# Hand-written instruction orders changed at six places of a two-block transformer kernel

## The reference

```python
# first block
h = h + 0.5 * swiglu(rmsnorm(h, ffn1_norm), ffn1_w_gate, ffn1_w_up, ffn1_w_down)   # hidden width 2816
u = rmsnorm(h, mix_norm)
(fq, fk, fv, ff, dq, dk, dv, iq, ik, iw, mq, g) = split(u @ w_in)
o_a = fox_attention(norm(fq), norm(fk), fv, log_sigmoid(ff + b_forget))   # 8 heads of 64, forget gates
o_b = dsa_attention(rope(norm(dq)), rope(norm(dk)), dv, rope(iq), rope(ik), iw, k_sel=128)
o_c = memory_attention(norm(mq), km, vm)       # 4 heads of 128; km, vm from 256 memory rows
h = h + sum_n(sigmoid(g_n) * (o_n @ w_branch[n])) @ w_out
h = h + 0.5 * swiglu(rmsnorm(h, ffn2_norm), ffn2_w_gate, ffn2_w_up, ffn2_w_down)
# second block
p = rms_norm(h, norm_mix_pre) @ w_in_2         # qa, ka, va, qb, kb, vb; 8 query heads, 2 key heads each
mixed = concat(group_norm(global_attention(qa, ka, va)), group_norm(window_attention(qb, kb, vb, sink)))
h = h + rms_norm(mixed @ w_out_2, norm_mix_post)
h = h + rms_norm(swiglu(rms_norm(h, norm_ffn_pre), w_gate_2, w_up_2, w_down_2), norm_ffn_post)
```

## Time and profile before

| | us |
|---|---|
| median of 3 runs (lowest, highest) | 2039.42 (2037.93, 2040.73) |
| the profiled execution, its own time | 2040.19 |
| its span in the trace | 2038.4 |
| PE busy, share of the span | 1960.4, 96% |
| POOL busy, share | 1468.2, 72% |
| DVE busy, share | 949.7, 47% |
| ACT busy, share | 516.1, 25% |

### The profile page before, as it was taken

How to read it: one execution, slowest core, us unless ns; L and a number is a source line. 1 busy time by engine, 2 the same in 40 slices (tenths; PEclk the granted TensorE clock), 3 DMA queues, 4 the chain that set the end, 5 groups by cost and what they waited for, 6 DMA issues and landing times.

```text
span 2038.4 us, 25930 instructions
## 1 busy us (share of the span) xinstructions
PE 1960.4 (96%) x8919; PEld 1597.9 (78%) x8919; DVE 949.7 (47%) x1196; ACT 516.1 (25%) x941; POOL 1468.2 (72%) x1676
## 2 busy tenths in 40 slices
PE   7999999999999999999999999999999989999998
PEld 5788888777677887887788888886778768888886
DVE  6532340488666469656432331017775574323101
ACT  3211100244345342333211110012555441111001
POOL 5777777778666667856777777766665768777776
PEclk9999999999999999999999999999999989999999
DMA  5333323232211223212333332324010013333332
GB/s 170 93 93 98 98 93 98 74 87 84 72 43 53 73 63 93 73 32 63 93 93 93 95 100 94 101 83 103 21 29 24 21 52 100 95 95 100 103 102 74
DMA packets 256183, 164.45 MB, mean 81 GB/s; under 512 B 30204, under 2 KB 245310, under 8 KB 255982
## 3 DMA queue, kind: packets, MB, share of 16 engines
q1 hardware_dynamic: 254304, 157.90, 26.6%
q10 hardware_dynamic: 1806, 5.58, 0.8%
HBM read 161.33 MB, written 2.13 MB: 80 GB/s over the span
## 4 chain that ended last, share of the span: by engine, by line
PE 80%; DVE 9%; POOL 4%; issue 3%; ACT 2%; ACTq 1%; DMA 0%; DVEq 0%; POOLq 0%
PE bank L920 12%; PE bank L922 12%; PE bank L921 12%; PE bank L1222 4%; PE bank L1223 4%; PE bank L1224 4%; PE bank L1040 4%; PE bank L1041 4%; PE bank L1042 4%; POOL w_lo L703 2%; PE bank L1118 2%; PE bank L1035 2%; PE bank L1036 2%; PE bank L1037 2%; DVE work L2582 2%
## 5 line engine op out<-in xcount | busy, mean ns | idle before, releaser
L703 POOL TENSOR_TENSOR w_lo<-raw,w_hi 128x256 fp32r<-128x256 f32 x1088 | 866.3, 827 | 22.7
L699 POOL TENSOR_SCALAR w_hi<-raw 128x1024 fp32r<-128x1024 f32 x272 | 294.5, 1083 | 356.0 <-PE bank L922 153.6
L920 PE MATMUL bank<-u_hi,w_hi 128*128 128x512 f32 x1040 | 407.8, 392 | 3.8 <-DVE u_lo L2436 2.9
L921 PE MATMUL bank<-u_lo,w_hi 128*128 128x512 f32 x1040 | 405.7, 390 | 0.0
L922 PE MATMUL bank<-u_hi,w_lo 128*128 128x512 f32 x1040 | 405.7, 390 | 0.0
L920 PEld LDWEIGHTS bank<-u_hi,w_hi 128*128 128x128 f32 x1040 | 195.8, 188 | 47.0 <-issue 4.2
L921 PEld LDWEIGHTS bank<-u_lo,w_hi 128*128 128x128 f32 x1040 | 195.9, 188 | 41.4 <-issue 0.7
L922 PEld LDWEIGHTS bank<-u_hi,w_lo 128*128 128x128 f32 x1040 | 195.8, 188 | 40.6
L1222 PE MATMUL bank<-u_hi,w_hi 128*128 128x512 f32 x464 | 193.9, 418 | 2.7 <-POOL w_lo L703 1.4
L1223 PE MATMUL bank<-u_lo,w_hi 128*128 128x512 f32 x464 | 183.3, 395 | 0.0
L1224 PE MATMUL bank<-u_hi,w_lo 128*128 128x512 f32 x464 | 183.2, 395 | 0.0
(11 more groups left out here) (555 smaller groups left out, 3573.3 us busy)
## 6 DMA issues: line engine op xcount, KB each, us to landing
raw<-in_w_in SPq DMA_DIRECT2D x52, 512.0 KB, 3.7
raw<-in_ffn_w_gate SPq DMA_DIRECT2D x44, 512.0 KB, 3.8
raw<-in_ffn_w_up SPq DMA_DIRECT2D x44, 512.0 KB, 3.8
raw<-in_ffn_w_down SPq DMA_DIRECT2D x44, 512.0 KB, 3.4
raw<-in_w_gate SPq DMA_DIRECT2D x22, 512.0 KB, 3.8
raw<-in_w_up SPq DMA_DIRECT2D x22, 512.0 KB, 3.8
raw<-in_w_down SPq DMA_DIRECT2D x22, 512.0 KB, 3.3
raw<-in_w_branch SPq DMA_DIRECT2D x12, 512.0 KB, 3.5
```

Source lines behind the costliest of these rows:

```text
L699: pool.tensor_scalar(w_hi[:, s, :], raw[:, k, :], 1.0, 1.0, ALU.mult, ALU.mult).then_inc(hi_done, 1)
L703: pool.tensor_tensor(w_lo[:, s, c], raw[:, k, c], w_hi[:, s, c].bitcast(F32), ALU.subtract).then_inc(low_quarter if quarter < 3 else split ...
L920: pe.matmul(outs[:, 0:n], wh, rhs_hi[:, c, :], start=(c == 0), stop=False)
L921: pe.matmul(outs[:, 0:n], wh, rhs_lo[:, c, :], start=False, stop=False)
```

## The change

Six places of the order change; the arithmetic stays, and so do nearly all instructions.

1. **Last pair of the down projection** (first and second feed-forward). The order over (m, k) was (4..7, 0), then (0, 0), (0, 1), (1, 0), (1, 1), (2, 0), (2, 1), (3, 0), (3, 1), then (4..7, 1). Now it is (4, 5, 6, 7, 0, 1; 0), (0, 1), (2, 0), (3, 0), then (1..7; 1). A product with k = 1 waited for its whole weight tile, and now waits for the quarter that it reads. In the first feed-forward the last two `m_lo` wait for one more finished unit.
2. **Memory slots.** In slots 2 and 3 `by_cos` and `both` of the single key move from between the low halves to behind the next slot's maxima and diagonal. Six of the eight cleared half tiles move from slot 2 to the end of slot 0.
3. **Branch and output projection.** `dsa_branch` takes its first sixteen products with two outputs x ahead of the two others. `w_out_a` takes its units one after the other and no longer interleaves the first two. `mix_lo` lies in another place, over `o_lo`, so that it does not lie where `u_lo` of chunks 4 to 7 is written, and those are made as their residuals come. The feed-forward behind it waits for `res` 6 and no longer 8.
4. **Second block's first panels.** Three products of qa0 stand between chunk 5 and chunk 6 of ka. On DVE the reciprocal for a1 stands ahead of `value_low`.
5. **Second block's attention.** `both` of a3 and of a4 stand ahead of the reciprocal of their step; PE's hook 13 is now 12, and 17 is now 18; ACT's and DVE's pieces for a4 move along.
6. **Third feed-forward's start.** The matmuls of chunk 0 that need only u_hi come first, in both panels, and the second panel follows one chunk behind, no longer two. DVE makes `u_lo` of chunk 0 and 1 earlier, between the residual additions.

The rows below are an engine's instructions in program order, with the line, the operation, out<-in and what it waits for.

DVE, memory slot 3, before: `m_kl` and `m_vl` are low halves that PE waits for, `prep_tmp` is by_sin's result, `rowmax` are the maxima.

The diff, cut to its changed lines (left out: the forget sums on ACT wait for 3 cleared groups, and the second place where `mix_lo` is indexed by `MIX_LO`):

```diff
@@ -246,7 +246,8 @@
-        mix_lo = at("mix_lo", [P, KC, S], u_at + 24576, F32R)
+        mix_lo = at("mix_lo", [P, 12, S], o_at, F32R)
+        MIX_LO = 0, 1, 2, 3, 8, 9, 10, 11
@@ -982,14 +983,26 @@
-                for c in range(KC):
+
+                def first_chunk():
+                    pe.wait_ge(n_hi, SPLITS[ni] * KC + 1)
+                    for k in range(2):
+                        weights(u + k, 0)
+                        b, slot = bank[banks[k]], slots[k]
+                        pe.matmul(b[:], w_hi[:, slot, 0:P], u_hi[:, 0, :], start=True, stop=False)
+                        pe.matmul(b[:], w_lo[:, slot, 0:P], u_hi[:, 0, :], start=False, stop=False)
+                    pe.wait_ge(n_lo, SPLITS[ni] * KC + 1)
+                    for k in range(2):
+                        pe.matmul(bank[banks[k]][:], w_hi[:, slots[k], 0:P], u_lo[:, 0, :], start=False, stop=False)
+                first_chunk()
+                residual_turned(0)
+                for c in range(1, KC):
...
-                        chunk(1, c - 2)
+                        chunk(1, c - 1)
                     residual_turned(c)
-                for c in range(KC - 2, KC):
-                    chunk(1, c)
+                chunk(1, KC - 1)
@@ -1064,13 +1077,16 @@
-                    order = [(m, 0) for m in range(4, KC)] + [(m, k) for m in range(4) for k in range(2)]
-                    order += [(m, 1) for m in range(4, KC)]
+                    order = [(m, 0) for m in (4, 5, 6, 7, 0, 1)] + [(0, 1), (2, 0), (3, 0)]
+                    order += [(m, 1) for m in range(1, KC)]
...
-                        pe.wait_ge(split_ready, d0 + FT)
                         pe.wait_ge(f_lo, fi * FT + FT)
+                        if fi == 2:
+                            pe.wait_ge(split_ready, d0 + FT)
+                    if k and fi < 2:
+                        weights(d0 + FT - 1, m)
@@ -1521,10 +1537,11 @@
-                for c in range(4):
+                order = [(x, c) for c in range(3) for x in range(2)] + [(2, 0), (3, 0), (0, 3), (1, 3)]
+                order += [(x, c) for c in range(1, 4) for x in (2, 3)]
+                for x, c in order:
                     pe.wait_ge(o_split, c + 1)
-                    for x in range(4):
-                        branch_mm(16 + x, c, bank[banks[x]][:])
+                    branch_mm(16 + x, c, bank[banks[x]][:])
@@ -1534,35 +1551,29 @@
-                b, slot = bank[m], m % SPL
+                b, slot = bank[m % 4], m % SPL
...
-                pe.matmul(b[:], wh, mix_lo[:, c, :], start=False, stop=False)
+                pe.matmul(b[:], wh, mix_lo[:, MIX_LO[c], :], start=False, stop=False)
...
-                pe.wait_ge(b_add, 16)
-                for c in range(KC - 2):
-                    pe.wait_ge(b_lo, c + 1)
-                    mix_mm(0, c)
-                for c in range(KC - 2):
-                    mix_mm(1, c)
-                for c in range(KC - 2, KC):
-                    pe.wait_ge(b_lo, c + 1)
-                    mix_mm(0, c)
-                for c in range(KC - 2, KC):
-                    mix_mm(1, c)
-                for m in range(2, KC):
-                    if m >= 4:
+                for m in range(KC):
+                    if m < 4:
+                        pe.wait_ge(b_add, 9 + (0, 1, 4, 5)[m])
+                    else:
                         pe.wait_ge(res, m - 3)
-                    panel(U_WO + m, m % SPL, m % 4, (mix_hi, mix_lo))
+                    for c in range(KC):
+                        if m == 0:
+                            pe.wait_ge(b_lo, c + 1)
+                        mix_mm(m, c)
...
-            pe.wait_ge(res, KC)
+            pe.wait_ge(res, KC - 2)
@@ -1624,9 +1635,13 @@
+                query = b2_panel("qa0")
+                next(query)
                 for c in b2_panel("ka"):
+                    if c == KC - 2:
+                        go_on(query, 3)
                     first_key(c)
-                for c in b2_panel("qa0"):
+                for c in query:
@@ -1680,8 +1695,8 @@
-                    13: lambda: aux_free("a3", lambda: sum_a(4, AUX)),
-                    17: lambda: (pe.wait_ge(h_std, H_B2 + 5), turn_a(4)),
+                    12: lambda: aux_free("a3", lambda: sum_a(4, AUX)),
+                    18: lambda: (pe.wait_ge(h_std, H_B2 + 5), turn_a(4)),
...
@@ -2357,9 +2372,8 @@
-                    14: lambda: (std_a(4, AUX), load_exp()),
-                    13: lambda: copy_b(2),
-                    18: lambda: high_a(4),
+                    13: lambda: (copy_b(2), std_a(4, AUX), load_exp()),
+                    19: lambda: high_a(4),
@@ -2700,6 +2714,8 @@
+                    if j == 2:
+                        dve.wait_ge(unit_done, U_GU1 + 3 * FT - 3)
@@ -2773,10 +2789,7 @@
-                by_cos, by_sin, both = rope_parts(R_PREP + j, x, 0, cos1[:], sin1[:], prep_tmp[:], x)
-                by_sin()
-                by_cos()
-                both()
+                return rope_parts(R_PREP + j, x, 0, cos1[:], sin1[:], prep_tmp[:], x)
@@ -2786,7 +2799,8 @@
-                    turn_key(i - 2)
+                    by_cos, by_sin, both = turn_key(i - 2)
+                    by_sin()
@@ -2818,8 +2832,8 @@
-                empty_halves(fst, ("qh", "ql", "kh", "kl")).then_inc(c_one, 1)
-                dve.wait_ge(c_one, 1)
+                empty_halves(fst, ("qh",)).then_inc(c_one, 1)
+                dve.wait_ge(c_one, 2)
@@ -2835,9 +2849,15 @@
+                if i >= 2:
+                    by_cos, by_sin, both = turn_key(i - 2)
+                    by_cos()
+                    both()
...
+                    dve.wait_ge(h_out, H_DK + 1)
+                    empty_halves(fst, ("ql", "kh", "kl")).then_inc(c_one, 1)
...
@@ -3042,10 +3062,9 @@
-                if 1 <= m <= 4:
+                if m:
                     gained_low(N_F2, G_F2, m - 1)
-            for c in range(4, KC):
-                gained_low(N_F2, G_F2, c)
+            gained_low(N_F2, G_F2, KC - 1)
@@ -3118,10 +3137,14 @@
+                dve.wait_ge(h_std, H_B2 + 2)
+                dve.reciprocal(HEAD_SQ[1], HEAD_SQ[1]).then_inc(h_rec, 1)
...
-                norm_a(1)
+                dve.wait_ge(h_rec, H_B2 + 2)
+                dve.scalar_tensor_tensor(out=raw_x[:, X_OF[1], :], in0=raw_x[:, X_OF[1], :], scalar=gain[:, G_QA:G_QA + 1],
+                                         in1=HEAD_SQ[1], op0=ALU.mult, op1=ALU.mult).then_inc(h_out, 1)
@@ -3170,16 +3193,16 @@
-                    (11, "end"): a3[2],
+                    (11, "start"): a3[2],
...
-                    (17, "mid"): a4[0],
-                    (17, "end"): a4[1],
-                    (18, "mid"): a4[2],
-                    (18, "end"): lambda: low_a(4),
+                    (18, "mid"): a4[0],
+                    (18, "end"): a4[1],
+                    (19, "start"): a4[2],
+                    (20, "start"): lambda: low_a(4),
@@ -3266,19 +3289,26 @@
-            for c in range(2):
-                b = bank[7 - 3 * c]
-                gained(c, b[:])
+
+            def added(c):
                 dve.wait_ge(n_t, SCALED[N_POST] * KC + c + 1)
-                dve.tensor_tensor(hT[:, c, :], hT[:, c, :], b[:], ALU.add).then_inc(x_ready, 1)
-            for c in range(2, KC + 3):
+                dve.tensor_tensor(hT[:, c, :], hT[:, c, :], bank[7 - 3 * c][:], ALU.add).then_inc(x_ready, 1)
+            gained(0, bank[7][:])
+            added(0)
+            gained(1, bank[4][:])
+            gained_low(N_FPRE, G_FPRE2, 0)
+            added(1)
+            gained(2, W[4])
+            gained_low(N_FPRE, G_FPRE2, 1)
+            gained(3, W[5])
+            third_square(1)
+            for c in range(4, KC + 3):
                 if c < KC:
-                    if c >= 4:
-                        dve.wait_ge(x_pool, c - 3)
+                    dve.wait_ge(x_pool, c - 3)
...
-                if c - 3 >= 1:
+                if c - 3 >= 2:
```

4 lines of the change are left out of this document (2 added, 2 removed).

## The result

| | before | after |
|---|---|---|
| median of 3 runs, us | 2039.42 (2037.93 to 2040.73) | 2023.24 (2019.71 to 2023.26) |
| the profiled execution | 2040.19 | 2023.26 |
| its span | 2038.4 | 2021.4 |

The account below looks back on a forecast made before the run. PE's matmul list was taken as the bound, with only its idle time and half clock removable. 1.9 + 6.3 + 4.8 + 3.8 + 3.2 + 1.2 = 21.2 gave a forecast of 2018.2 us, range 2012 to 2031.

Parts of the forecast that it names:

- rival (a): Whole kernel: waits shrink but the clock still falls at the three places; gain 14.8, 2024.6 us; chance 0.24.
- One sign of being wrong: Half clock stands where there was none; the other sign: PE's idle time in the six stretches falls by under 8 us.
- Part 1, 1.9 forecast: First feed-forward's end: 1.4 from two w_lo waits, plus 0.5 of 1.36 from the earlier split; bounds 0.7 and 2.8.
- the 5.1 of the sum: First feed-forward's end: the split taking the two moved m_lo lasts at most 1.43 + 2.81 + 0.84 = 5.1.
- Part 2, 6.3 forecast: Memory slots: 0.96 + 1.26 + 1.09 from three waits plus 3.0 for the clock; bounds 2.5 and 7.2.
- The clock's 3.0: Memory slots: with a wait of 0.9 left, the half clock from 517.50 should not come; 3.0 back.
- Part 3, 4.8 forecast: Branch and output projection: branch nothing net despite a new 1.5 wait, w_out's start 1.7, then 3.1; bounds 2.5 and 5.5.
- Part 4, 3.8 forecast: Second feed-forward's end: 2.1 from POOL reaching its splits earlier, 1.7 for the clock; bounds 1.2 and 4.5.
- Part 5, 3.2 forecast: Second attention: 7.3 of waits and clock, less remaining waits of 1.8 and 2.3; bounds 0 and 5.5.
- The clock term: Second attention: the half clock stretch behind the wait of 3.21 goes, 1.7 won.
- rival (b): Whole kernel: waits only move, as DVE's and POOL's chains set the pace; gain 8.0, 2031.4 us; chance 0.15.
- Part 6, 1.2 forecast: Third feed-forward's start: 0.7 from a shorter tail, 0.5 kept of starting 2 us earlier; bounds 0 and 2.0.

Follow-up runs that it names:

- experiment 3: The changed kernel run again with the same program, nothing altered: 2021.59 us, ratio 0.9917.
- experiment 2: Kernel before with m_lo's wait, cleared tiles, branch order, a1's reciprocal, part 6: 2029.99; with pair order, ropes behind maxima, w_out with mix_lo, part 5: 2028.63.
- experiment 4: Changed kernel with hooks 13, 21 and low halves ahead of reciprocal: 2019.55; only PE's half of part 6: 2019.55; no m_lo wait, tiles cleared in slot 2: 2025.91.
- experiment 1: Changed kernel with part 5 undone: 2021.92; changed kernel with a4's sum at hook 13 and b0's rotation at hook 21: 2019.88.
- experiment 5: Changed kernel with hooks 13, 21 and PE's half of part 6: 2018.20; without qa0's three products: 2022.07; with a4's sum at hook 13 alone: 2019.00.

## Why the prediction was right, and where it was not

The time lies in the range, and the sum was 4 to 5 us too large (21.2, against 17.0 of the span and 16.2 of the medians). The measured gain is nearer to rival (a), 14.8, than to the forecast, and the two are mixed in it: the waits shrank as forecast in parts 1 to 3, and the clock fell again in part 5. That the sum came as close as it did is partly luck, since part 1 gave 2.6 more than its term and part 5 4.1 less, and the untouched start and the fall near 1604 took 1.9 that no term had. One sign of being wrong came true: half clock stands near 1471 and near 1604, where there was none. The other did not: PE's idle time in the six stretches fell from 34 to 21 us, by more than 8. By its own steps:

- **Part 1, 1.9 forecast.** The mechanism was right, the second term mis-sized. The two waits of 1.4 gave 2.0, as each has a slow first matmul behind it. For the earlier split behind the pair I had counted 0.5 of 1.36, fearing DVE's e_lo; it gave 2.5. The split does start 1.36 earlier against PE, as forecast, and its w_hi and w_lo take 1.05 and 3.73, where before they took 1.43 and 4.83. The contention that I had held against the edit became less on POOL, and some of it went to DVE, whose e_lo grew longer and PE waits 0.2 for them. It is also what makes this part vary: 0.7 of the gain hangs on which of two instructions that start 0.04 us apart is stretched (experiment 3). The split beside the two moved m_lo, 373.51 to 378.25, took 4.7, below the 5.1 of the sum, and PE did not wait for it. The Trainium skill, page "SBUF — State Buffer", section "SBUF: two separate sides", says that a DVE instruction with two SBUF inputs and a POOL instruction that reads SBUF exclude each other for a whole instruction; by it the prediction's estimate was 5.6. The trace agrees that there is a cost, and it is smaller. But POOL's rows alone hide a part of it, here and in the 0.42 that the prediction read: these two m_lo took 2.14 on DVE, where two of 0.69 would be 1.38.

```profile
373.51 1.52 POOL L700 TENSOR_SCALAR w_hi<-raw 128x1024 fp32r<-128x1024 f32 x1 [0.71 <-PE bank L1055]
375.11 3.14 POOL L704 TENSOR_TENSOR w_lo<-raw,w_hi 128x256 fp32r<-128x256 f32 x4
373.42 2.14 DVE L2720 TENSOR_TENSOR m_lo<-mT,m_hi 128x512 fp32r<-128x512 f32 x2 [2.61 <-PE bank L1055]
```

- **Part 2, 6.3 forecast.** 7.5. All three waits went, I had left 0.9 of the second. The split between the pieces was wrong: I gave the waits of 0.96 and 1.09 to the ropes and 1.26 to the tiles, and experiment 2 shows that the tiles alone take 2.16 and 1.09 away and give 6.2, while the ropes are needed for the 0.96 only. The clock's 3.0 came back with either piece in experiment 2, but with the ropes alone a fall stood there in experiment 4.
- **Part 3, 4.8 forecast.** 5.0, with the new wait at 1.3 (1.5 forecast) and the 3.1 of w_out back in full; experiment 2 has 0.2 for the branch alone, which the prediction took as nothing.
- **Part 4, 3.8 forecast.** 3.0, but by other terms: 1.7 in the stage itself, as much as the one fall that went. PE's waits there come to the same, 3.3 before (0.8, 0.5, 0.6, 1.4) and 3.4 now (2.2 for u_lo, 1.2 for the squares' sum), so the splits' earlier start paid nothing here: the 2.1 of the sum failed. The other 1.3 is the reciprocal of a1, which the prediction left at nothing.
- **Part 5, 3.2 forecast.** This step failed. The hook for the sum waited 2.4, not 1.8: `both` takes 1.37 and not 0.68, so that it ends 3.1 earlier against PE's list, not 4.0.

```profile
1441.71 1.37 DVE L2546 TENSOR_TENSOR raw_x<-raw_x,turn_tmp 128x512 f32<-128x512 f32 x1
```

  The second wait was sized right, 2.4 for 2.3 forecast. The clock term, 1.7 won back, failed altogether: I took it that waits of 1.8 and 2.3 leave the clock up, and it fell at both. Behind them a third wait appears, for q2l or the maxima. Experiments 1, 4 and 5 show rival (b) at work: without a fall PE waits 6.7 us in this stage with part 5 (2.4, 2.4, 1.5, 0.4) and still 4.8 with both hooks later, where the two waits aimed at were 4.8 by themselves; with the low halves moved too it waits 4.2, beside one fall. That DVE's chain of maxima, rope and reciprocal sets the pace is argued from this: DVE is busy 30.45 of the 36 us from 1440 to 1476 with both hooks later, though no run made that chain shorter.
- **Part 6, 1.2 forecast.** The early start came (6.4 in place of 8.3 idle), the later chunks ate it. Experiment 4 shows the culprit: DVE's swap, which the prediction named as delaying all chunks by 0.9 and then judged to be just hidden.
- **Clock.** Rival (a) was right in kind: at part 5 and, in other executions, at parts 1, 2 and 4, falls come behind waits of 0.87 to 2.4. What the prediction took from three waits without a fall (1.8, 1.51 and 2.43), that waits of this length leave the clock up, has no ground: the same wait of 1.99 in the same place was followed by one or not.

Not settled: what decides whether the clock falls behind a given wait.

## What to carry to other kernels

Price a reordering stage by stage and check it by matching the nth matmul of both traces: the sum here was 4 us off while single stages were off by 4 and by 2.6 in opposite directions. Where one engine is nearly full in a stage, moving the other's hooks moves most of the wait on: of two waits of 2.4 aimed at in part 5, 1.8 came as time when both hooks went later. Work that can leave the busy stretch, as the cleared tiles did, gave more here (6.2). Compare stages only between executions with the same half clock stretches, and look at the single instructions where two engines stretch each other: which of them gives way can differ from one execution to the next.
